# Streaming encoder layer on one core: tile 1 routed beside rows 104 to 128 instead of 80 to 128, the projection beside rows 10 to 98, and V's rows up to row 112 added on VectorE

## What is computed

```
a = rmsnorm(h)
[q_d|k_d|v_d|q_s|k_s|v_s] = a @ w_in                    # 1024 x 3072
h += w_out(concat[diff_attn(q_d,k_d,v_d), stick_break(q_s,k_s,v_s)])
c = rmsnorm(h)
q = c @ w_query                                          # 8 heads x 2 halves x 128
s = q . sub_keys                                         # 128 keys to a half
# a head: the 16 best of 16 x 16 sums of the two halves' 16 best
coef = softmax(top) * gelu(c . expert_u[idx])            # 8 heads x 16 experts to a token
h += sum over the 128 experts of coef * expert_v[idx]
h += (p @ w_ple) * sigmoid(rmsnorm(h) @ w_pgate)
y = rmsnorm(h)
```

## Time and profile before

| | |
|---|---|
| median of three runs | 4168.78 us |
| profiled execution | 4159.01 us, span 4157.2 us |
| TensorE busy | 3313.0 us, 80% of the span |
| VectorE busy | 2908.4 us, 70% |
| GpSimd busy | 2764.6 us, 67% |
| ScalarE busy | 1173.0 us, 28% |
| moved from and to HBM | 1369 MB, mean 329 GB/s |
| chain that ended last | PE 39%, POOL 22%, DMA 12%, DVE 11%, issue 10%, ACT 5% |

### The profile page before, as it was taken

One profiled execution on the slowest core, in us unless ns is written; L12 is line 12 of the kernel. 1 busy time (PEld: TensorE's weight loads), 2 busy tenths in 40 slices (PEclk: granted clock), 3 DMA queues, 4 the chain that ended last, 5 costly groups with the idle time before them and its releaser, 6 DMA issues.

```text
span 4157.2 us, 32609 instructions
## 1 busy us (share of the span) xinstructions
PE 3313.0 (80%) x9404; PEld 1589.7 (38%) x9404; DVE 2908.4 (70%) x5623; ACT 1173.0 (28%) x2269; POOL 2764.6 (67%) x2355
## 2 busy tenths in 40 slices
PE   7869996778877887887788788868897787758877
PEld 3434443234324333443444244424442342323333
DVE  2276764867787687769776878687768476687775
ACT  2312321143124213421451145115521243111111
POOL 0014545777777777877787777777677566667774
PEclk9989998989999999899999999999999898879998
DMA  5347779899999999999998999999999899899995
GB/s 199 110 138 273 268 266 357 314 377 390 341 364 380 351 358 360 368 342 357 370 352 331 353 374 344 336 351 367 330 362 354 307 354 362 316 330 385 380 387 218
DMA packets 452609, 1369.16 MB, mean 329 GB/s; under 512 B 47697, under 2 KB 118225, under 8 KB 451409
## 3 DMA queue, kind: packets, MB, share of 16 engines
q0 software_dynamic: 331776, 1208.11, 77.7%
q1 hardware_dynamic: 95312, 135.89, 9.2%
q10 hardware_dynamic: 25344, 23.07, 1.6%
HBM read 1338.57 MB, written 28.31 MB: 329 GB/s over the span
## 4 chain that ended last, share of the span: by engine, by line
PE 39%; POOL 22%; DMA 12%; DVE 11%; issue 10%; ACT 5%; ACTq 0%; SPq 0%; POOLq 0%; DVEq 0%
PE sum_ps L844 13%; POOL v_ring L664 11%; POOL u_ring L647 11%; PE z_ps L787 7%; PE z_ps L739 6%; DMA v_ring<-expert_v_in,idx_tile 5%; DMA u_ring<-expert_u_in,idx_tile 4%; DVE u_ring L1570 3%; PE sum_ps L739 3%; PE z_ps L877 2%; DVE arena L1664 1%; DVE neg_max L1766 1%; PE out_ps L904 1%; DMA arena<-g_ffn_in 1%; PE z_ps L1151 1%
## 5 line engine op out<-in xcount | busy, mean ns | idle before, releaser
L844 PE MATMUL sum_ps<-v_ring,diag 128*128 128x512 f32 x3196 | 1701.9, 669 | 602.4 <-DMA v_ring<-expert_v_in,idx_tile 395.9
L647 POOL DMA_INDIRECT u_ring<-expert_u_in,idx_tile x1152 | 1374.1, 1193 | 709.6 <-DVE dots L1570 353.9
L1570 DVE CUSTOM_DVE_ANT_0 u_ring<-u_ring,c_rows 128x1024 f32<-128x1024 f32 x1152 | 1405.7, 1226 | 581.3 <-DMA u_ring<-expert_u_in,idx_tile 568.6
L664 POOL DMA_INDIRECT v_ring<-expert_v_in,idx_tile x1152 | 1340.5, 1164 | 351.2 <-issue 324.3
L844 PEld LDWEIGHTS sum_ps<-v_ring,diag 128*128 128x128 f32 x3196 | 620.8, 209 | 1427.0 <-issue 795.2
L1584 DVE SCALAR_TENSOR_TENSOR acc<-v_ring,coef,acc 128x1024 f32<-128x1024 f32 x344 | 442.5, 1286 | 9.6 <-DMA v_ring<-expert_v_in,idx_tile 9.5
L1227 ACT ACTIVATE diag<-ident,coef 128x128 f32<-128x128 f32 x799 | 288.8, 394 | 526.7 <-PE sum_ps L844 478.8
L787 PE MATMUL z_ps<-weights,arena 128*128 128x512 f32 x768 | 342.5, 599 | 3.9 <-ACT arena L1189 2.2
L739 PE MATMUL z_ps<-weights,arena 128*128 128x512 f32 x576 | 261.5, 605 | 7.3 <-DVE c_rows L1872 3.7
L787 PEld LDWEIGHTS z_ps<-weights,arena 128*128 128x128 f32 x768 | 146.4, 193 | 183.1 <-issue 175.8
L1310 ACT ACTIVATE arena<-z_ps,neg_max 128x128 f32<-128x128 f32 (+7 forms) x128 | 94.7, 740 | 419.3 <-DVE neg_max L1766 419.2
(11 more groups left out here) (192 smaller groups left out, 3029.2 us busy)
## 6 DMA issues: line engine op xcount, KB each, us to landing
u_ring<-expert_u_in,idx_tile POOLq DMA_INDIRECT x1152, 6.4
v_ring<-expert_v_in,idx_tile POOLq DMA_INDIRECT x1152, 6.4
weights<-w_in_in SPq DMA_DIRECT2D x6, 2048.0 KB, 16.6
u_ring<-w_query_in SPq DMA_DIRECT2D x16, 512.0 KB, 4.8
weights<-w_out_in SPq DMA_DIRECT2D x2, 4096.0 KB, 24.5
weights<-w_query_in SPq DMA_DIRECT2D x1, 8192.0 KB, 52.5
qk_turned<-arena ACTq DMA_DIRECT2D x24, 256.0 KB, 6.2
arena<-x_all_in SPq DMA_DIRECT2D x9, 512.0 KB, 7.0
```

The lines of the kernel that those rows point to most:

```text
L647: pool.indirect_dma_start(u_rows[r % U_RING][:, :], None, ins["expert_u"], bass.IndirectOffsetOnAxis(ap=idx_tile[:, e % 2, at:at + 1], axis=0)
L664: pool.indirect_dma_start(v_rows[g % V_RING][:, :], None, ins["expert_v"], bass.IndirectOffsetOnAxis(ap=idx_tile[:, e % 2, at:at + 1], axis=0)
L844: mm = nc.tensor.matmul(sum_ps[:, half * W:(half + 1) * W], diag[:, by_tensor[g] % DIAGS, :], v_rows[g % V_RING][:, half * W:(half + 1) * ...
L1570: nc.vector.tensor_tensor_reduce(row, row, c_rows[e % 2][:, :], 1.0, 0.0, ALU.mult, ALU.add, dots[:, s % 2, r % TOP:r % TOP + 1]).then_inc ...
```

## The change

```
-FIRST_ATTENDED, FIRST_ROUTED = 12, 80
-PACE = ((-ROWS, 27), (-64, 52), (-60, 53), (-51, 54), (-38, 54), (0, 58), (10, 75), (FIRST_ROUTED - 6, 2 * USES * T))
+FIRST_ATTENDED, FIRST_ROUTED = 12, 104
+PACE = ((-ROWS, 27), (-64, 52), (-60, 53), (-51, 54), (-38, 54), (0, 58), (10, 75), (76, 173),
+        (FIRST_ROUTED - 6, 2 * USES * T))
...
-    if 0 < step < 5:
+    if 0 < step < 7:
         return tuple(range(15))
     if step < 8:
-        return ((1, 3, 5, 7, 9, 11, 13), (5, 11), ())[step - 5] if step else ()
+        return ()
```

## The result

The changed kernel took 4172.38 us, the median of 20 runs (4152.92 to 4178.42), against 4157.31 us for the kernel before in 20 runs beside it (4147.96 to 4170.25): a ratio of 1.0026, 95% interval 1.0016 to 1.0037. So it is a little slower, within the 0.3% that count as no change, where a gain of 20 us was forecast. The first three runs of the kernel before had given 4168.78; the larger number of runs puts it 11 us lower, at its profiled execution.

What follows compares the result with a forecast made beforehand. Bounds: TensorE in the projection of tiles 3 to 8, DMA while w_out and w_query land, VectorE from there to row 128. Terms 12 - 5 - 27 = -20 us, so 4168.8 - 20 = 4149 us; range 4126 to 4174.

Steps and rivals of the forecast that it cites:

- Stage A, +12: Projection of tiles 3 to 8, 322.6 us before, TensorE the bound: 12 us longer, from +3.8 to +31.
- upper bound of +31: Projection of tiles 3 to 8 if the DMA reaches only a share of 0.85: 353 us.
- terms 3.8 and 11: Projection of tiles 3 to 8: 3.8 us for two more V rows on TensorE, 11 for DMA competition up to row 76.
- Stage A's rows: Projection of tiles 3 to 8 now ends near row 99 instead of 79: 20 rows more, not 24.
- Stage B, -5: Loading w_out and w_query, 57.5 us before, DMA full: four gathers fewer, 5 us shorter, between 0 and -10.
- Stage C, -27: Rest of tile 1's routing and rows up to 128, 142.5 us before, VectorE the bound: 27 us shorter, from -16 to -34.
- the -2: From the tokens to the first search, 32.7 us before: 2 us shorter, mostly from two V rows gone between the queries.
- VectorE comes late to its handovers: Rival: tile 1's attention handovers make TensorE wait, projection of tiles 3 to 8 +58, total +26, 4195 us; chance 0.16.
- The DMA takes the place of TensorE: Rival: DMA bounds the projection of tiles 3 to 8 at a share of 0.85; 4168 us, no change; chance 0.20.
- GpSimd becomes the bound: Rival: gathers wait for VectorE's dots and additions, projection of tiles 3 to 8 +65, total +33, 4202 us; chance 0.02.
- All is covered: Rival: projection of tiles 3 to 8 only +3.8, later stretches at their good ends; -40, 4129 us; chance 0.15.

Runs made afterwards that it cites:

- experiment 1: Changed kernel with VectorE taking tile 1's four attention maxima one or two rows earlier; 4127.31 us, ratio 0.9927 to the kernel before.
- experiment 10: The same kernel as experiment 1, measured again on another chip in more runs; 4144.08 us, ratio 0.9968 to the kernel before.
- experiment 5: Kernel before, without the change, with tile 1's attention maxima taken earlier on VectorE; 4158.16 us, ratio 1.0008 to the kernel before.
- experiment 4: Changed kernel with an even projection pace from row 10 to 98 and tile 1's attention over 80 rows instead of 64; 4165.31 us, ratio 1.0027.
- experiment 9: Changed kernel with tile 1's attention sixteen rows later, at rows 28 to 92 instead of 12 to 76; 4166.18 us, ratio 1.0022.
- experiment 7: Changed kernel with tile 1's attention maxima earlier and the projection pace even from row 10 to 98; 4141.97 us, ratio 0.9956.
- experiment 8: Changed kernel with tile 1's attention maxima earlier and that attention eight rows later; 4144.17 us, ratio 0.9975.

## Why the prediction was wrong

Its own test said: wrong if the projection ends after 650. It ended at 674.5. The sign was wrong by one term.

**Stage A, +12: this step failed.** It measured +46, beyond its upper bound of +31. The step took the length from TensorE's work and the DMA's capacity, and priced their competition by a DMA share of 0.92. The DMA was at 0.82: it did not bind. In no run did TensorE wait directly for the DMA in A beyond single waits of up to 4.2 us. The work was right: the two rows of V cost 3.7 us where 3.8 were reckoned. That A measured 334.0 and 336.7 with the maxima out of the way (experiments 1 and 10), for a forecast of 334.6, is partly luck: the 8 us that the forecast gave to the DMA are there in the main TensorE's 8.4 us at the attention's transposes. The sum itself was loose. Its terms 3.8 and 11 make 14.8, not 12; and attention and V took 44 us of TensorE by the groups of the kernel before, not 30, which leaves 7 of the 11. What was left out, and put at nothing, is TensorE's wait in the attention, which comes of the order within VectorE's stream: 22.5 us at the scores, and 32 to 35 us of the stage in all (experiments 10 and 1). The forecast read that TensorE had waited 3.7 us for VectorE and concluded that the handovers had room; but that was true of the old meeting places, and the change moved them. The numbers for it stood in the kernel: 98 halves beside 66 rows give a tile 16 rows, and an attention step has 16. The mark named in the prediction, TensorE's wait for VectorE under 10 us, would even have passed: directly it is 1.0 us, because in the attention ScalarE stands between the two, and the wait carries its name.

**Stage A's rows.** 20 more rows were forecast beside A; 104 dots instead of 79 began before its end, 25 more. In experiment 1 there were 104 as well, at 638.4 us. So the stage held five rows more than I gave it.

**Stage B, -5: right in size by luck** (-5.4). Five gathers of each kind were issued in it where ten were the earlier trace rows and eight were forecast. Ten gathers fewer would be worth 12.5 us by the forecast's own 420 GB/s; so the reason was larger and its worth smaller than reckoned.

**Stage C, -27: right** (-29.7). The 16 dots and the U waits went as worked out, -26.1 for -25 from the first search on. Row 128 did not come later (1.55 us of wait, not 4), and the scores gained 1.6 us more than the -2.

**The rivals.** "VectorE comes late to its handovers" had the right place and sign; its price came from waits for U, which were 14.1 us in all of A, and not from the rotation ahead of the maxima. "The DMA takes the place of TensorE" falls with the share of 0.82, though its time, 4168, is near the result. "GpSimd becomes the bound" falls: the gathers' means are 1,195 and 1,081 ns (1,220 and 1,096 before), and GpSimd waited 84.7 us for dots. "All is covered" is excluded by the idle time of 46 us.

**Open.** All kernels with the later routing start stage A 1 to 4 us later than the 302.4 of before; the kernel of experiment 5 does so too (304.3), so it is not of the change alone. Of the 46 us, 27 are idle time and 4 the rows of V; the other 15 are the same matmuls taking longer at a lower mean granted clock (268.7 us for the projection's 576 instead of 261.5, for one), which came back with the idle time in experiment 1. Experiments 4 and 9 part the two: TensorE is idle 38 us in the stage there, not far below the 43 of the changed kernel, but busy only 318 and 317 us instead of 326, at 0.97. So the amount of idle time does not set this loss by itself; what does is open. Open, too, is which order makes the waits at the attention's transposes, and why the rows after 128, which no edit touches, differ by up to 26 us between the profiles. And the gains of the single edits do not add up in the total (experiments 7, 8).

## What to carry to other kernels

When two repeating streams are laid beside each other, compare their periods before their sums: equal periods turn a meeting that would happen now and then, or never, into one that happens every time. Within an in-order stream, put what others wait for and what is already computable ahead of an instruction that itself has to wait. And read a wait along the whole ring of engines: the one that TensorE names here is ScalarE, the one to mend is VectorE.

## What the runs showed of the hardware

A wait can cost TensorE twice, but does not always. In stage A of the changed kernel its mean granted clock was 0.94, where it was 0.98 before and in experiment 1, and the 16 scores of the attention's second kind (L878, qs) took 535 ns each instead of 380. Behind a wait of 3.38 us, in the changed kernel and then in experiment 9:

```profile
398.11 1.22 PE L878 MATMUL z_ps<-arena,qs 128*128 128x256 f32 x2 [3.38 <-ACT arena L1311]
...
399.55 9.17 PE L740 MATMUL z_ps<-weights,arena 128*128 128x512 f32 x16
```

```profile
379.42 0.70 PE L878 MATMUL z_ps<-arena,qs 128*128 128x256 f32 x2 [3.38 <-ACT arena L1311]
...
380.18 7.03 PE L740 MATMUL z_ps<-weights,arena 128*128 128x512 f32 x16
```

Sixteen matmuls of the projection took 9.17 us in the one and 7.03 in the other; the mean granted clock was 0.73 from 398.1 to 408.6 us and 1.00 from 379.4 to 387.3. What made the difference is not shown.

I had also expected GpSimd's gathers to grow longer, if at all, beside VectorE's added work; they did not.
